# Block 1 without barriers around its recurrence, GELU beside the last set, and 14 of 16 gate matmuls behind the state inputs

## The chip, the cores and the metric

One core of one Trainium2 chip runs the whole program in one launch. The metric is the device time of that core in microseconds. The engines are TensorE (PE), VectorE (DVE), ScalarE (ACT), GpSimd (POOL) and SyncE (SP); each runs its own instruction stream and they meet only through semaphores. DMAs are issued from SP, ACT and POOL.

## What is computed

The model has three blocks on an activation of 1024 positions by 1024 channels, float32. The change lies in the first mixer of block 1, an S5 layer. Cut to what matters:

```
h = rmsnorm(x, norm_g[0])
branch, gate = split(h @ s5_w_in)            # 1024 -> 2 x 1024
# 64 groups of 16 channels drive 64 complex states each
h_t = lam_bar * h_{t-1} + b_bar @ u_t        # diagonal recurrence over 1024 positions
y_t = Re(C h_t) + D * u_t
y = gelu(y)
y = y * sigmoid(y @ s5_w_glu + s5_b_glu)
x = x + (y * silu(gate)) @ s5_w_out
```

What follows (the gating block, then block 2 with delta-rule and attention mixers, then block 3) is the same in both kernels.

## The kernel before

All activations are held transposed, channels on the partitions: eight tiles of 128 x 1024 in `c.X` (residual), `c.B` (normed input, later the GELU output y) and `c.C` (gate). One work area `c.W` is cut anew by every phase; its first 8192 columns are also `c.D`, eight tiles. A product of 1024 x 1024 by the activation is eight groups; a group is one output tile, made by 16 matmul instructions (eight k, two halves of 512 columns; each stands as two records in the trace) in `product_ct` (matmul at L161). Groups alternate between two halves of the PSUM tensor `products`: `start_group` waits until the group two before has been read (`group_read`), `take_group` waits until a group is done. Weights come in blocks of 512 KB through a ring of eight slots. SP's queue issues block n + 8 when the last group that uses block n is done.

The program is a list of phases. Every engine runs through the list in order. A phase added with `meet=True` ends in a barrier (L3568): each of the four compute engines drains, adds one to `phase_end` and waits for all four.

Four phases matter:

- **Norm.** `rms_phase` writes `c.B`.
- **`s5_input_phase`** (barrier behind it). ACT's queue loads the parameters. TensorE makes the eight branch tiles from `s5_w_in`, then turns C by eight transposes (L601) into one more group, `gp`. ACT copies each branch tile into one of four staging tiles (L617, the order of columns changed), then copies C (L620, L621). POOL stores each staged tile to `branch_dram` (L627) and at the end waits for all stores. VectorE makes b_bar, the powers of lam_bar, and a table of phases E in `c.C` (last of it at L636).
- **`s5_scan_phase`** (barrier behind it). The 64 groups go in eight sets of eight. The 1024 positions are cut into 128 steps of eight, so that a set needs one scan of 128 steps. For each set i: VectorE makes two filters, Pm and Q (L887, then `s5_pq_done`). TensorE transposes Pm (L827; ACT copies it to `into`, L867) and makes the kernel within eight steps from b_bar and Q (L839; ACT copies it to KK, L872). VectorE adds D on the diagonal (L942). POOL stores KK and loads it back eight times into the triangular `within` (L805, L809). TensorE makes the state inputs X from `into` and U (L847). U is the branch, loaded by POOL from `branch_dram` in eight DMAs a set (L792). VectorE turns X by E, scans (L953), turns back into H and signals `s5_h_done`; it goes on to the filters of set i + 1. TensorE meanwhile makes gate tile i (16 matmuls), then waits for H and `within` and makes the outputs (L857, L859). ACT copies them to Y (L878), which TensorE's next transposes wait for, and writes Silu of the gate tile to `c.C` (L880). POOL stores Y in eight DMAs (L814). At the end POOL waits for all stores of Y.
- **`s5_gate_phase`.** ACT's queue loads y back into `c.D` in four DMAs of two tiles (L985), ACT applies GELU to eight tiles into `c.B` (L992), TensorE waits for all eight, makes the eight GLU groups; ACT applies sigmoid (L997), VectorE multiplies `c.C` by y (L1014) and by the sigmoid (L1018, `s5_gated`); TensorE waits for all eight and makes the eight output groups.

Of the kernel before, what the change touches and what calls it, by code (L numbers as in the profile page):

```python
# [11 lines left out]
ACT = mybir.ActivationFunctionType  # L12
# [4 lines left out]
P = 128  # L17
# [133 lines left out]
def product_ct(c, pe, g, blocks, acts, ready=None):  # L151
# [12 lines left out]
    last.then_inc(c.group_done, 1)  # L164
# [386 lines left out]
def s5_input_phase(c, t, normed):  # L551
# [3 lines left out]
    b0 = len(c.plan.blocks)  # L555
    for m in range(KT):
        c.plan.add_blocks(columns(c, t["s5_w_in"][0], P * m, 1), g0 + m)
    c.plan.groups += KT
    gp = c.plan.groups
    c.plan.groups += 1  # L560
# [29 lines left out]
    def tensor(pe):  # L590
# [4 lines left out]
        for m in range(KT):  # L595
            product_ct(c, pe, g0 + m, [(b0 + m, KT, P)], [c.B[:, k, :] for k in range(KT)], normed if m == 0 else None)
        out = start_group(c, pe, gp)
        pe.wait_ge(c.s5_c_loaded, 16 * 16)
        for n in range(2):
            for q in range(4):  # L600
                last = pe.transpose(out[:, (4 * n + q) * P:(4 * n + q + 1) * P], craw[:, n, q, :], c.ident[:, :])  # L601
        last.then_inc(c.group_done, 1)

    def scalar(act):
# [8 lines left out]
        for m in range(KT):  # L613
            if m >= 4:
                act.wait_ge(c.branch_stored[m % 4], 16)
            got = take_group(c, act, g0 + m).rearrange("p (n s) -> p n s", s=S5_T)
            act.activation(stage[:, m % 4, :].rearrange("p (s n) -> p n s", s=S5_T), got, ACT.Copy)\  # L617
               .then_inc(c.group_read[(g0 + m) % 2], 1)
        got = take_group(c, act, gp)
        act.activation(s.CT[:, 0].rearrange("p j h -> p (j h)"), got[:, 0:BANK], ACT.Copy)  # L620
        act.activation(s.CT[:, 1].rearrange("p j h -> p (j h)"), got[:, BANK:], ACT.Copy, scale=-1.0)\  # L621
           .then_inc(c.group_read[gp % 2], 1)

    def gpsimd(pool):
        for m in range(KT):
            taken(c, pool, g0 + m)
# [120 lines left out]
def s5_scan_phase(c, t):  # L747
# [25 lines left out]
    Pm = area(2, JC, S5_T, S5_H)  # L773
    into = area(2, JC, P)
    Q = [area(2, JC, S5_T + 1, S5_H) for _ in range(2)]
    within = area(GC, S5_T * S5_H)
    KK = area(GC, S5_T * S5_H)
    r8 = area(JC, S5_N)
    U = [area(GC, S5_N) for _ in range(2)]
    T = area(2, JC, S5_N)  # L780
    Hh = area(2, JC, S5_N)
# [13 lines left out]
    def gpsimd(pool):  # L795
        pool.memset(within[:, :, :], 0.0).then_inc(c.pool_step, 1)
# [19 lines left out]
        pool.wait_ge(c.s5_y_stored, 16 * S5_T * S5_C)  # L816

    def tensor(pe):
        for i in range(S5_C):
            q = Q[i % 2]  # L820
            pe.wait_ge(c.s5_pq_done, i + 1)
# [19 lines left out]
            last.then_inc(c.s5_turned, 1)  # L841
            pe.wait_ge(c.s5_into_ready, 2 * i + 2)
# [7 lines left out]
            product_ct(c, pe, g0 + i, [(b0 + i, KT, P)], [c.B[:, k, :] for k in range(KT)])  # L850
# [10 lines left out]

    def scalar(act):
        for i in range(S5_C):
# [10 lines left out]

            act.wait_ge(c.s5_y_done, i + 1)
# [4 lines left out]
            act.activation(c.C[:, i, :], take_group(c, act, g0 + i), ACT.Silu).then_inc(c.group_read[(g0 + i) % 2], 1)  # L880

    def vector(dve):
# [5 lines left out]

        ch.done(dve.memset(H[:, :, :, 0:1], 0.0))
# [80 lines left out]
def s5_gate_phase(c, t):  # L970
# [8 lines left out]
    raw, y, gate = c.D, c.B, c.C  # L979
# [3 lines left out]
    def loads(sp):  # L983
        for m in range(0, KT, 2):
            sp.dma_start(raw[:, m:m + 2, :], c.y_dram[m * P:(m + 2) * P, :].rearrange("(k p) n -> p k n", p=P))\  # L985
              .then_inc(c.s5_y_loaded[m // 2], 16)

    def scalar(act):
        for m in range(KT):
            act.wait_ge(c.s5_y_loaded[m // 2], 16)  # L990

            act.activation(y[:, m, :].rearrange("p (n s) -> p s n", s=S5_T),  # L992
                           raw[:, m, :].rearrange("p (s n) -> p s n", s=S5_T), ACT.Gelu_apprx_tanh).then_inc(c.s5_y_gelu, 1)
# [8 lines left out]
    def tensor(pe):  # L1002
        pe.wait_ge(c.s5_y_gelu, KT)
        for m in range(KT):
            product_ct(c, pe, g0 + m, [(b0 + m, KT, P)], [y[:, k, :] for k in range(KT)])
        pe.wait_ge(c.s5_gated, KT)
        for m in range(KT):
            product_ct(c, pe, g0 + KT + m, [(b0 + KT + m, KT, P)], [gate[:, k, :] for k in range(KT)])
# [12 lines left out]
    phase = Phase(loads=loads, tensor=tensor, scalar=scalar, vector=vector)  # L1021
# [2351 lines left out]
def build(nc, t, out):  # L3373
    with ExitStack() as ctx:
# [165 lines left out]
        then(s5_input_phase(c, t, norm.normed), meet=True)  # L3540
        then(s5_scan_phase(c, t), meet=True)
# [124 lines left out]
```

## Time and profile before

| | us |
|---|---|
| Median of 3 runs | 4367.71 (4366.61 to 4369.51) |
| Profiled execution | 4361.82 |
| Its span | 4359.2 |
| TensorE busy | 4018.6 (92%) |
| VectorE busy | 1616.3 (37%) |
| ScalarE busy | 865.4 (20%) |
| GpSimd busy | 427.8 (10%) |

Times in the views are counted from the start of the span. The input phase of the mixer runs from about 50 to 178 us, the scan phase from 178 to 452, the gate phase from 452 to about 700. A bracket at the end of a timeline row tells how long the engine had been idle before and what ended the wait.
### The profile page before, as it was taken

The page shows a single profiled execution, that of the slowest core. Times are in us where ns is not written, and L with a number is a line of the kernel's source. Part 1 is how long each engine was busy: PE and PEld are TensorE (multiplying, and loading weights), DVE is VectorE, ACT ScalarE, POOL GpSimd, SP SyncE. Part 2 cuts the span into 40 slices and gives each one's busy share as a digit, 9 for nine tenths or more (in the row PEclk, how much of TensorE's full clock was granted, in tenths as well). Part 3 has the DMA queues.
Part 4 walks back from the last instruction along what each step waited for, and adds up shares of the span by engine and source line. Part 5 has one row for each costly group of instructions (what it writes and reads, how often), then busy time and mean ns, then how long its engine had stood idle before and what let it go on. Part 6 is the DMA issues. An engine that isn't in the chain of part 4 may idle for free.

```text
span 4359.2 us, 32122 instructions
## 1 busy us (share of the span) xinstructions
PE 4018.6 (92%) x13135; PEld 2033.6 (47%) x13135; DVE 1616.3 (37%) x2310; ACT 865.4 (20%) x971; POOL 427.8 (10%) x496
## 2 busy tenths in 40 slices
PE   5899699999999899987889999999989999989997
PEld 2455243454334567544434444444435554444553
DVE  6466113210233454134131434343443654324333
ACT  2111202200145221234120000000042431221122
POOL 0143000000000122012000222222200000000000
PEclk8999899999999999998999999999999999989998
DMA  4222111211101101110001111111111101003101
GB/s 117 66 66 55 64 38 40 53 29 39 34 15 34 40 24 40 34 49 20 27 20 51 39 48 39 48 39 49 39 29 25 29 14 35 20 13 97 29 10 44
DMA packets 291104, 174.49 MB, mean 40 GB/s; under 512 B 24096, under 2 KB 281999, under 8 KB 290703
## 3 DMA queue, kind: packets, MB, share of 16 engines
q1 hardware_dynamic: 253008, 126.47, 10.5%
q0 software_dynamic: 9856, 23.87, 2.0%
q10 hardware_dynamic: 28094, 22.11, 1.8%
q8 instruction: 105, 1.72, 0.2%
q14 instruction: 41, 0.33, 0.0%
HBM read 159.20 MB, written 13.21 MB: 40 GB/s over the span
## 4 chain that ended last, share of the span: by engine, by line
PE 53%; DVE 3%; ACT 2%; issue 1%; DMA 0%; POOL 0%; ACTq 0%; DVEq 0%
PE products L161 11%; PE products L278 9%; PE others L278 9%; PE products L2565 8%; PE products L2578 3%; PE others L2644 2%; PE products L1778 1%; PE products L179 1%; PE products L405 1%; PE products L1941 1%; PE others L1972 1%; PE products L1787 1%; PE products L3093 1%; PE products L3092 1%; PE others L1191 1%
## 5 line engine op out<-in xcount | busy, mean ns | idle before, releaser
L161 PE MATMUL products<-normed,weights 128*128 128x512 f32 x1728 | 759.1, 600 | 46.5 <-ACT normed L992 36.3
L161 PEld LDWEIGHTS products<-normed,weights 128*128 128x128 f32 x1728 | 330.7, 193 | 460.0 <-issue 451.1
L161 PE MATMUL products<-gate,weights 128*128 128x512 f32 x768 | 331.6, 593 | 5.0 <-DVE gate L1018 2.5
L2565 PE MATMUL products<-normed,weights 128*128 128x512 f32 (+2 forms) x704 | 321.8, 608 | 5.0 <-DVE normed L391 5.0
L161 PE MATMUL products<-residual,weights 128*128 128x512 f32 x672 | 295.6, 598 | 8.2 <-ACT residual L464 6.2
L161 PEld LDWEIGHTS products<-gate,weights 128*128 128x128 f32 x768 | 145.9, 190 | 188.9 <-issue 182.3
L161 PEld LDWEIGHTS products<-residual,weights 128*128 128x128 f32 x672 | 128.3, 192 | 170.6 <-issue 163.7
L2565 PEld LDWEIGHTS products<-normed,weights 128*128 128x128 f32 (+2 forms) x704 | 126.6, 187 | 163.9 <-issue 161.8
L179 PE MATMUL products<-weights,normed 128*128 128x512 f32 x384 | 167.5, 599 | 5.0 <-DVE normed L391 5.0
L278 PE MATMUL products<-gate,s_small 128*128 128x512 f32 x320 | 139.9, 592 | 0.0
L3361 POOL DMA_DIRECT2D out_dram<-work x8 | 4.3, 542 | 1214.3 <-ACT work L3350 1209.5
L1576 POOL TENSOR_TENSOR work<-work,levels 128x512 f32<-128x512 f32 x8 | 10.2, 1272 | 1130.7 <-DVE work L1702 1130.7
L179 PEld LDWEIGHTS products<-weights,normed 128*128 128x128 f32 x384 | 73.6, 192 | 99.3 <-issue 96.5
L288 POOL TENSOR_TENSOR s_small<-weights 128x512 f32<-128x512 f32 x32 | 41.4, 1295 | 798.0 <-PE products L161 305.9
L2644 PEld LDWEIGHTS others<-work 128*128 128x128 f32 (+1 forms) x1024 | 94.3, 195 | 47.8 <-issue 38.2
L1778 PE MATMUL products<-residual,weights 128*128 128x512 f32 x256 | 115.9, 600 | 0.0
L2644 PE MATMUL others<-work 128*128 128x128 f32 (+1 forms) x1024 | 98.7, 283 | 18.1 <-DVE work L2837 6.2
L1029 DVE TENSOR_TENSOR residual<-products,residual 128x1024 f32<-128x1024 f32 x24 | 29.4, 1224 | 229.0 <-PE products L161 220.2
L2578 PE MATMUL products<-weights,normed 128*128 128x512 f32 x256 | 111.5, 594 | 0.0
L161 PE MATMUL products<-work,weights 128*128 128x512 f32 x224 | 100.3, 605 | 4.9 <-DVEq L3568 4.9
L278 PEld LDWEIGHTS products<-gate,s_small 128*128 128x128 f32 x320 | 60.9, 190 | 76.4 <-issue 76.4
L2837 DVE COPY_PREDICATED work<-levels,others 128x1024 f32<-128x1024 int32 x56 | 73.0, 1304 | 39.2 <-PE others L2644 34.8
(543 smaller groups left out, 5641.9 us busy)
## 6 DMA issues: line engine op xcount, KB each, us to landing
weights<-in_w_in_dram SPq DMA_DIRECT2D x83, 512.0 KB, 3.8
weights<-in_w_up_dram SPq DMA_DIRECT2D x32, 512.0 KB, 4.2
weights<-in_w_down_dram SPq DMA_DIRECT2D x32, 512.0 KB, 5.0
weights<-in_sgu_w_in_dram SPq DMA_DIRECT2D x24, 512.0 KB, 3.8
weights<-in_s_w_in_dram SPq DMA_DIRECT2D x16, 512.0 KB, 4.0
weights<-in_w_out_dram SPq DMA_DIRECT2D x24, 256.0 KB, 2.9
work<-in_x_dram ACTq DMA_DIRECT2D x8, 512.0 KB, 10.1
branch_scratch<-work POOLq DMA_DIRECT2D x8, 512.0 KB, 2.9
```

Of the source, the lines that this page charges most:

```text
L161: last = pe.matmul(out[0:cols, half * BANK:(half + 1) * BANK], slot(c, b, kt, cols)[:, k, :], acts[n][:, half * BANK:(half + 1) * BANK], s ...
L179: last = pe.matmul(out[:, q * P:q * P + BANK], acts[k][:, tile * P:(tile + 1) * P], wide[:, :, k, :], start=(k == 0), stop=(k == KT - 1))
L278: last = pe.matmul(self.bank[n], w[:, k * P:(k + 1) * P], moving[k], start=(k == 0), stop=(k == KT // 2 - 1))
L405: last = pe.matmul(out[:, h * BANK:(h + 1) * BANK], c.mean_mat[:, :], c.tmp[:, k % 2, h * BANK:(h + 1) * BANK], start=(k == 0), stop=(k == ...
L1191: last = pe.matmul(out[:, h * BANK:(h + 1) * BANK], c.mean_mat[:, :], squares[:, h * BANK:(h + 1) * BANK], start=True, stop=True)
L1778: last = pe.matmul(o[:, 0:BANK], slot(c, f.b, KT, P)[:, kk, :], x[kk][:, half * BANK:(half + 1) * BANK], start=(kk == 0), stop=(kk == KT - 1))
L1787: last = pe.matmul(o[:, 0:BANK], x[kk][:, f.n * P:(f.n + 1) * P], wide[:, :, kk, :], start=(kk == 0), stop=(kk == KT - 1))
L1941: pe.matmul(L[e][:, x:y], q[half(e), a, i * P:(i + 1) * P], k[half(e), a, x:y], start=True, stop=(y < w))
L2565: last = pe.matmul(out[0:cols, half * BANK:(half + 1) * BANK], slot(c, f.b, kt, cols)[:, kk, :], acts[kk][:, half * BANK:(half + 1) * BANK ...
L2578: last = pe.matmul(out[:, 0:BANK], x[kk][:, f.n * P:(f.n + 1) * P], wide[:, :, kk, :], start=(kk == 0), stop=(kk == KT - 1))
L2644: last = pe.matmul(pair(j + h)[:, i * P:(i + 1) * P], K[rows(u, h), i * P:(i + 1) * P], Q[rows(u, h), i * P:(i + 1) * P], start=True, stop ...
L2837: ch.done(dve.copy_predicated(o, mask, got), *reader(j))
```

## The change

Both barriers around the scan phase are dropped. What they ordered is ordered by waits and by a new layout of `c.W`:

- In the input phase the group `gp` with the turned C moves from the end to between branch products 3 and 4, on TensorE and ACT, and the group numbers are shifted accordingly. In the scan VectorE waits for C's copy, ACT and POOL for the stores of the branch, and POOL clears `within` only when set 0's filters are done.
- The work area of the scan is laid out so that the parts that set 7 still uses (Q[1], U[1], `within`, H, Y) lie behind the first seven tiles of `c.D`.
- In the scan, the gate product of set i is issued by a generator: one matmul before the wait for the filters, one after the kernel products, 14 behind the state inputs. The number of matmuls is the same.
- In the last set, ACT waits for H, then issues the loads of y's tiles 0 to 6 in three DMAs, takes Silu of the last gate tile and GELU of tiles 0 to 2, and only then copies the outputs to Y. GELU of tiles 3 to 7 follows. Tile 7 is loaded by POOL behind its own stores.
- In the gate phase TensorE waits for one GELU tile at a time in the first GLU group, and for one gated tile at a time in the first output group.

```diff
@@ product_ct
-                pe.wait_ge(c.normed, ready + n + 1)
+                pe.wait_ge(c.normed if on is None else on, ready + n + 1)
@@ s5_input_phase
+    gm = [g0 + m + (1 if m >= 4 else 0) for m in range(KT)]
+    gp = c.s5_c_group = g0 + 4
...
         for m in range(KT):
-            product_ct(c, pe, g0 + m, ..., normed if m == 0 else None)
-        out = start_group(c, pe, gp)
-        pe.wait_ge(c.s5_c_loaded, 16 * 16)
-        for n in range(2):
-            for q in range(4):
-                last = pe.transpose(...)
-        last.then_inc(c.group_done, 1)
+            if m == 4:
+                out = start_group(c, pe, gp)
+                ...                               # the same eight transposes
+            product_ct(c, pe, gm[m], ..., normed if m == 0 else None)
@@ scalar: the two copies of C move to m == 4 likewise
@@ s5_scan_phase, layout of c.W
     Pm = area(2, JC, S5_T, S5_H)
+    T = area(2, JC, S5_N)
+    Q = [area(2, JC, S5_T + 1, S5_H)]
+    r8 = area(JC, S5_N)
     into = area(2, JC, P)
+    Hh = area(2, JC, S5_N)
+    KK = area(GC, S5_T * S5_H)
+    U = [area(GC, S5_N)]
     within = area(GC, S5_T * S5_H)
+    U.append(area(GC, S5_N))
+    Q.append(area(2, JC, S5_T + 1, S5_H))
     H = area(2, JC, S5_N)
     Y = area(GC, S5_N)
@@ gpsimd
+        pool.wait_ge(c.s5_pq_done, 1)
         pool.memset(within[:, :, :], 0.0).then_inc(c.pool_step, 1)
...
         pool.wait_ge(c.s5_y_stored, 16 * S5_T * S5_C)
+        pool.dma_start(c.D[:, KT - 1, :], c.y_dram[(KT - 1) * P:KT * P, :]).then_inc(c.s5_y_loaded[3], 16)
@@ tensor
+    def gates(pe):
+        for i in range(S5_C):
+            out = start_group(c, pe, g0 + i)
+            block_ready(c, pe, b0 + i)
+            for k in range(KT):
+                for half in range(HALVES):
+                    last = pe.matmul(...)
+                    if k < KT - 1 or half < HALVES - 1:
+                        yield
+            last.then_inc(c.group_done, 1)
+            yield
...
+            advance(1)
             pe.wait_ge(c.s5_pq_done, i + 1)
...                                               # transposes, kernel products
+            advance(1)
             pe.wait_ge(c.s5_into_ready, 2 * i + 2)
...                                               # state inputs
-            product_ct(c, pe, g0 + i, [(b0 + i, KT, P)], [c.B[:, k, :] for k in range(KT)])
+            advance(14)
             pe.wait_ge(c.s5_h_done, i + 1)
@@ scalar
+    def gelu(act, m):
+        act.wait_ge(c.s5_y_loaded[min(m // 2, 2) if m < KT - 1 else 3], 16)
+        act.activation(c.B[:, m, :]..., c.D[:, m, :]..., ACT.Gelu_apprx_tanh).then_inc(c.s5_y_gelu, 1)
+
     def scalar(act):
+        for k in range(4):
+            act.wait_ge(c.branch_stored[k], 32)
...
+            if i == S5_C - 1:
+                act.wait_ge(c.s5_h_done, S5_C)
+                act.wait_ge(c.s5_y_stored, 16 * S5_T * i)
+                act.wait_ge(c.s5_kk_stored, 16 * S5_C)
+                for n, (lo, hi) in enumerate(((0, 2), (2, 4), (4, KT - 1))):
+                    act.dma_start(c.D[:, lo:hi, :], c.y_dram[lo * P:hi * P, :]...)\
+                       .then_inc(c.s5_y_loaded[n], 16)
+                act.activation(c.C[:, i, :], take_group(c, act, g0 + i), ACT.Silu).then_inc(...)
+                for m in range(3):
+                    gelu(act, m)
             act.wait_ge(c.s5_y_done, i + 1)
...
+        for m in range(3, KT):
+            gelu(act, m)
@@ vector
+        taken(c, dve, c.s5_c_group)
+        ch.wait()
@@ s5_gate_phase: its loads and its GELU loop are gone
-        pe.wait_ge(c.s5_y_gelu, KT)
         for m in range(KT):
-            product_ct(c, pe, g0 + m, [(b0 + m, KT, P)], [y[:, k, :] for k in range(KT)])
-        pe.wait_ge(c.s5_gated, KT)
+            product_ct(c, pe, g0 + m, [(b0 + m, KT, P)], [y[:, k, :] for k in range(KT)],
+                       0 if m == 0 else None, c.s5_y_gelu)
         for m in range(KT):
-            product_ct(c, pe, g0 + KT + m, ..., [gate[:, k, :] for k in range(KT)])
+            product_ct(c, pe, g0 + KT + m, ..., [gate[:, k, :] for k in range(KT)],
+                       0 if m == 0 else None, c.s5_gated)
@@ build
-        then(s5_input_phase(c, t, norm.normed), meet=True)
-        then(s5_scan_phase(c, t), meet=True)
+        then(s5_input_phase(c, t, norm.normed))
+        then(s5_scan_phase(c, t))
```

## Rows read from the trace of the kernel before

**Rows 1.** The page, busy time of each engine with its share.
```profile
PE 4018.6 (92%) x13135; PEld 2033.6 (47%) x13135; DVE 1616.3 (37%) x2310; ACT 865.4 (20%) x971; POOL 427.8 (10%) x496
```

**Rows 2.** Stretches: length, busy of each engine (instructions), granted clock, DMA share, GB/s.
```profile
197.10:219.30 22.20, 22.20 (x82) 12.61 (x80) 20.67 (x34) 0.00 (x0) 4.19 (x8) 1.00 0.17 41
219.30:228.10 8.80, 6.47 (x73) 5.03 (x72) 0.56 (x2) 5.26 (x5) 7.39 (x15) 0.81 0.45 90
435.50:471.80 36.30, 0.00 (x1) 0.00 (x0) 8.61 (x8) 18.36 (x12) 4.16 (x8) 0.51 0.38 130
471.80:488.40 16.60, 16.57 (x33) 7.29 (x34) 1.19 (x1) 1.24 (x1) 0.00 (x0) 0.84 0.00 0
```

**Rows 3.** The barriers' line: POOL's drains, duration ns min/median/max.
```profile
L3568 POOLq DRAIN  x7: 41/1399/8962, 177.5 to 3134.7; - x7
```

**Rows 4.** Timeline, input to set 0: start us, us, engine, line, work, [idle before].
```profile
60.14 112.06 PE L161 MATMUL products<-normed,weights 128*128 128x512 f32 x256
172.04 1.04 PE L601 MATMUL products<-ident,work 128*128 128x128 f32 x8
...
117.31 1.98 ACT L617 ACTIVATE work<-products 128x1024 f32<-128x1024 f32 x1 [11.75 <-PE products L161]
...
174.51 0.53 POOL L627 DMA_DIRECT2D branch_scratch<-work  x1 [13.19 <-ACT work L617]
...
179.58 8.39 POOL L792 DMA_DIRECT2D work<-branch_scratch  x16 [0.30 <-POOL work L796]
...
178.30 0.07 DVE L889 MEMSET work<- 128x8 f32 x1 [47.48 <-POOLq L3568]
```

**Rows 5.** Timeline, set 0 to 1 on TensorE, VectorE, POOL; kernel products of set 7.
```profile
220.56 1.47 PE L827 MATMUL others<-ident,work 128*128 128x128 f32 x8 [1.21 <-ACT work L878]
221.96 3.15 PE L839 MATMUL others<-work,s_small 64*16 64x128 f32 x32
226.23 1.97 PE L847 MATMUL others<-work 128*64 128x128 f32 x32 [1.12 <-ACT work L872]
228.13 14.00 PE L161 MATMUL products<-normed,weights 128*128 128x512 f32 x32
...
228.25 2.87 DVE L887 TENSOR_TENSOR work<-others,gate 128x512 f32<-128x512 f32 x4 [1.44 <-PE others L847]
...
237.93 1.41 DVE L887 TENSOR_TENSOR work<-work 128x508 f32<-128x508 f32 x2
...
248.86 0.88 DVE L887 TENSOR_TENSOR work<-work 128x256 f32<-128x256 f32 x2
...
231.47 4.18 POOL L809 DMA_DIRECT2D work<-within_scratch  x8 [1.93 <-DMA within_scratch<-work]
...
407.84 2.39 PE L839 MATMUL others<-work,s_small 64*16 64x128 f32 x32
```

**Rows 6.** Timeline, last set to the first GLU product.
```profile
435.54 1.02 ACT L878 ACTIVATE work<-others 128x1024 f32<-128x1024 f32 x1 [24.25 <-PE others L859]
...
436.85 4.16 POOL L814 DMA_DIRECT2D y_scratch<-work  x8 [17.08 <-ACT work L878]
451.72 2.06 ACTq L985 DMA_DIRECT2D work<-y_scratch  x4
...
456.64 15.09 ACT L992 ACTIVATE normed<-work 128x1024 f32<-128x1024 f32 x8 [1.54 <-DMA work<-y_scratch]
...
471.83 3.75 PE L161 MATMUL products<-normed,weights 128*128 128x512 f32 x4 [36.33 <-ACT normed L992]
```

**Rows 7.** DMA issues, 170 to 480 us: issue, count, KB each, median us to landing.
```profile
work<-branch_scratch POOLq DMA_DIRECT2D x64, 64.0 KB, 2.6
...
y_scratch<-work POOLq DMA_DIRECT2D x64, 64.0 KB, 2.3
...
branch_scratch<-work POOLq DMA_DIRECT2D x1, 512.0 KB, 2.9
```

**Rows 8.** Timeline, first group of the output product.
```profile
587.07 13.14 PE L161 MATMUL products<-gate,weights 128*128 128x512 f32 x30 [2.52 <-DVE gate L1018]
```

More of the change, by code:

```diff
@@ L595, in tensor @@
         for m in range(KT):
-            product_ct(c, pe, g0 + m, [(b0 + m, KT, P)], [c.B[:, k, :] for k in range(KT)], normed if m == 0 else None)
-        out = start_group(c, pe, gp)
-        pe.wait_ge(c.s5_c_loaded, 16 * 16)
-        for n in range(2):
-            for q in range(4):
-                last = pe.transpose(out[:, (4 * n + q) * P:(4 * n + q + 1) * P], craw[:, n, q, :], c.ident[:, :])
-        last.then_inc(c.group_done, 1)
+            if m == 4:
+                out = start_group(c, pe, gp)
+                pe.wait_ge(c.s5_c_loaded, 16 * 16)
+                for n in range(2):
+                    for q in range(4):
+                        last = pe.transpose(out[:, (4 * n + q) * P:(4 * n + q + 1) * P], craw[:, n, q, :], c.ident[:, :])
+                last.then_inc(c.group_done, 1)
+            product_ct(c, pe, gm[m], [(b0 + m, KT, P)], [c.B[:, k, :] for k in range(KT)], normed if m == 0 else None)
     def scalar(act):
@@ L816, in gpsimd, with advance @@
         pool.wait_ge(c.s5_y_stored, 16 * S5_T * S5_C)
+        pool.dma_start(c.D[:, KT - 1, :], c.y_dram[(KT - 1) * P:KT * P, :]).then_inc(c.s5_y_loaded[3], 16)
[5 more added lines that the diff above has]
+                for half in range(HALVES):
+                    last = pe.matmul(out[:, half * BANK:(half + 1) * BANK], slot(c, b0 + i, KT, P)[:, k, :],
+                                     c.B[:, k, half * BANK:(half + 1) * BANK], start=(k == 0), stop=(k == KT - 1))
+                    if k < KT - 1 or half < HALVES - 1:
+                        yield
+            last.then_inc(c.group_done, 1)
+            yield
     def tensor(pe):
+        work = gates(pe)
+        def advance(n):
+            for _ in range(n):
+                next(work)
         for i in range(S5_C):
             q = Q[i % 2]
+            advance(1)
             pe.wait_ge(c.s5_pq_done, i + 1)
@@ L978, in s5_gate_phase @@
     c.plan.groups += 2 * KT
-    raw, y, gate = c.D, c.B, c.C
+    y, gate = c.B, c.C
     sig = c.tmp
     sums = Sums(c)
[L983 to L986, printed above, removed]
     def scalar(act):
[L989 to L993, printed above, removed]
         for m in range(KT):
@@ L1002, in tensor @@
     def tensor(pe):
[L1003 removed]
         for m in range(KT):
[L1005 to L1006 removed]
+            product_ct(c, pe, g0 + m, [(b0 + m, KT, P)], [y[:, k, :] for k in range(KT)],
+                       0 if m == 0 else None, c.s5_y_gelu)
         for m in range(KT):
[L1008 removed]
+            product_ct(c, pe, g0 + KT + m, [(b0 + KT + m, KT, P)], [gate[:, k, :] for k in range(KT)],
+                       0 if m == 0 else None, c.s5_gated)
     def vector(dve):
@@ L1019, in vector @@
         add_to_residual(c, dve, g0 + KT, sums)
-    phase = Phase(loads=loads, tensor=tensor, scalar=scalar, vector=vector)
+    phase = Phase(tensor=tensor, scalar=scalar, vector=vector)
     phase.sums = sums
```

36 lines of the change are left out of this document (17 added, 19 removed).

## The prediction

> **What bounds the kernel now.** I read the page first: TensorE is busy 92% of the span [rows 1], so only stretches in which it idles, or runs at the lower clock, can give time back. The mean by stages then shows where block 1 stands apart [rows 2]: TensorE works 22.2 of 22.2 us at the full clock through one set's gate product and output products, 6.47 of 8.80 us in the turn to the next set at a granted clock of 0.81, and not at all in the 36.3 us after the last set, after which the first GLU product takes 16.6 us at 0.84. Elsewhere such a product takes 13.85 us (14.00 less the modelled tail of the last matmul) [rows 5]. The rest of the program is not touched and moves along as a whole.
>
> Last I followed the time order of each engine through the three places where block 1 waits: input to set 0 [rows 4], one set to the next [rows 5], last set to the GLU products [rows 6]. The POOL row of the barriers' line gives the size of one hidden cost: one of its drains takes 8962 ns [rows 3].
>
> **Input to set 0.** Before: the last input product ends at 172.2, its copy is stored from 174.51, VectorE starts set 0's filters only at 178.30 after 47.48 us of waiting for POOL's drain, and the gate product of set 0 starts at 197.1. After: VectorE finished the phase tables at 130.8 (178.30 - 47.48 [rows 4]) and C is read by about 120.5, so the filters (10.4 us, as below) are ready near 141, far ahead. What is late next is the branch. The turn of C (1.04 us [rows 4]) now stands between input products 3 and 4. It also costs a wait: product 4 reuses product 3's bank pair, whose copy runs 117.31 to 119.25, while TensorE is through with C at 118.2. So 1.04 + 1.05 = 2.1 us is put on the chain: last store at 176.6 instead of 174.51. It lands 2.9 later [rows 7], 179.5; then memset and gap as before (1.3, from 178.30 to 179.58), first branch load 180.8, the eighth issued 7 x 0.53 = 3.7 later, landed after 2.6 [rows 7]: 187.1. ScalarE's two copies (from 179.5, 2 us) and POOL's wait for the filters lie inside that; set 0's kernel store waits behind 16 loads, until 189.3, and its way home (1.93 + 4.18 + 2.0 = 8.1 us [rows 5]) ends at 197.9, before the output products at 202. State inputs run 187.2 to 189.2 (1.97 us), 8.0 us ahead of 197.1. Of the gate product only 14 of 16 matmuls stand behind them: 2 x 0.866 = 1.73 saved. But TensorE has been idle some 8 us by then, so I charge the cold start that the first GLU product shows, 16.6 - 13.85 = 2.75. Sum: 8.0 + 1.7 - 2.7 = **7.0 us**. Bounds: without the cold start 9.7; with state inputs at half speed as well (another 2) 5.
>
> **Seven set-to-set rounds.** A round lasts (435.45 - 219.36)/7 = 30.87 us (ends of the output products, from the starts of what follows them [rows 5, 6]) and TensorE is in all of it: 13.85 gate, 8.4 outputs (22.2 - 13.85), 1.20 waiting for ScalarE's copy of the outputs, 1.40 transposes, 3.15 kernel products, 1.12 waiting for ScalarE's copy of these, 1.9 state inputs [rows 2, 5]. The change puts one gate matmul (0.87 us) into each wait. They fit: 0.87 < 1.12. That alone takes 1.73 off. The second part is the clock: 219.3 to 228.1 was granted 0.81, and once TensorE does not stop there, the dip may go. Transposes at the full clock took 1.04 [rows 4] against 1.47, and the kernel products in the one set that met the dip late took 2.39 against 3.15 [rows 5]: up to 1.2 us more, so a round of 27.9.
>
> VectorE's chain is the floor under that: 11.1 us from state inputs to state (228.25 to 239.34), 10.3 for the next filters (239.44 to 248.86 + 0.88), then 1.1 transposes, 1.9 to 2.4 kernel products, 1.0 copy and 2.0 state inputs, with handovers 27.7 us. The state itself (11.1) must be there when 14 matmuls (12.1) are through: it is, by 1.0 us, and that is what 16 less 2 leaves. POOL: its kernel rows landed at 237.6 (231.47 + 4.18 + 2.0) when the outputs started at 242; of those 4.4 us 3 are taken, 1.4 are left. So all three chains are within 1.5 us of each other, and I take 28.4 for a round, nearer the floor than 29.1. 7 x 2.5 = **17.5 us**. Bounds: 7 x 1.7 = 12 (dip stays) to 7 x 3.1 = 22 (floor); below 12 only if a late row or state is waited for, which these margins exclude as a rule.
>
> **Last set to GLU.** Before: outputs done 435.45, stores issued from 436.85, last one issued 3.6 later and landed after 2.3 [rows 7], 442.8; the loads are issued at 451.72, which is the 8.96 us drain [rows 3, 6]. First GELU 456.64, eight take 15.09, TensorE starts at 471.83 and ends product 0 at 488.4: 52.95 us after the outputs.
> After, counted from the end of the last set's state inputs: state 11.1; three loads issued by ScalarE, the first landed 4.92 later (451.72 to 456.64), 16.0. In between Silu (1.02, at 12.2 when the gate product is through) and one table load (1.28) are hidden. GELUs 0 to 2: 3 x 1.89, 21.7. Outputs end at 12.1 + 8.4 = 20.5, and the copy of Y waits behind those GELUs until 21.7 (1.2 late, the price of this order). From that copy's start 7.25 us to the last landing (435.54 to 442.8): 29.0; POOL's load of the last tile, 512 KB like the branch stores that took 2.9 [rows 7]: 32.0. GELUs 3 to 6 end at 30.3 beside it, GELU 7 at 33.9. TensorE follows tile by tile and has 14 of product 0's 16 matmuls behind it by about 32.2; two more after the last GELU, and 1 us for a short stop before: 36.6, or 16.1 after the outputs. 52.95 - 16.1 = **36.9 us** (of it 9.0 the drain, 2.7 the cold clock, 12.1 product 0 ahead, 13 the loads and GELUs beside the set). Bounds: 38.5 with the copy of Y in time and no stop; 27 if POOL keeps its 9 us.
> VectorE's eight gate multiplications (L1014) follow the GELUs and end 1.3 us after the last, long before the first sigmoid's product. SP issues the same weight loads on the same groups.
>
> A rule to hold against this: POOL's seven drains took 41 ns at least, 1399 in the median and 8962 at most [rows 3]. The Trainium skill, "VectorE: DVE Perf Modes", section "The DRAIN you can't avoid", knows the drains of the runtime's preamble as some 12 ns each, constant. By that a barrier costs nothing and the 9 us would belong to something else that stays; the median row is a hundred times that, so I count the 9 us as the barrier's; by the page the sum would be 54.9 and the time 4313.
>
> **GLU to output product.** TensorE waits 2.52 us for the last gated tile [rows 8]; with a wait per tile seven others stand before it: **2.5 us** (2 to 3).
>
> **Sum.** 7.0 + 17.5 + 36.9 + 2.5 = 63.9 us. The profiled execution took 4361.8 (span 4359.2 and 2.6 around it) and becomes 4297.9; the median of the three runs is 5.9 higher, 4367.7, so I predict 4304.
>
> **Rivals.**
> The clock's dip stays: gate matmuls fill 0.87 of each wait but transposes and kernel products run as slow as now. For it: the dip is there in every round though the wait is only 1.2 us. Against: that wait shrinks to 0.3. Rounds of 29.1: 17.5 becomes 12.3, so 4309.
> POOL keeps its 9 us: the long drain is work owed for its 64 x 3 DMA issues, and now stands in front of the load of the last tile. For it: the drain before it, with 8 issues behind it, was much shorter, as the store of 174.51 and the load of 179.58 enclose it. Against: in every round POOL issues its kernel loads as soon as the store before them has landed, 1.93 us [rows 5], with no debt to be seen. TensorE would then idle 11 us more and meet the cold clock (2.7): 4304 + 9 + 2.7 = 4316.
> Slower: the scattered gate matmuls fail to hold the clock and sets run at the half level. Gate matmuls then take 27.4 instead of 13.7 a set, 110 us over eight: 4304 + 110 = 4414. It outweighs the gain from 64/13.7 = five such sets on. Against: output products follow the gate matmuls now as then, at 1.00 [rows 2].
> The change doesn't do what it says: the last set's loads cannot start early because the stores of the set before are late. They land near 2 us after its state inputs, nine before they are needed; no chance of its own.
>
> **How the numbers follow.** Forecast 0.68, dip stays 0.16, POOL's 9 us 0.10, slower 0.03, the remaining 0.03 on losses that I do not see and that eat the gain. All low terms give 5 + 12 + 27 + 2 = 46 (4322), all high ones 9.7 + 22 + 38.5 + 3 = 73 (4295); both ends at once are unlikely, so the range is 4295 to 4321, and the forecast's own 4297 to 4311. 0.2% is 8.7 us, the least that counts as a difference here. Faster 0.95, same 0.02, slower 0.03.
>
> **What would show it.** Input: copy of C at about 119, TensorE idle 1 us there; filters of set 0 before 142; state inputs at 187, not 195. Rounds: a period of 28.4 and a granted clock near 1.00 in the turn; with 0.81 there and 29.1 the dip stayed. TensorE waiting for VectorE's state or for POOL's kernel rows would mean that a margin of 1.0 or 1.4 us was wrong. End: first GELU before the outputs end, the last load of Y's rows 32 us after the state inputs, product 0 finished 16 us after the outputs. The forecast is wrong if POOL stands still between the landed stores and that load, if a round stays above 29.5, or if anything after block 1 gives back time.

## The result

| | before | changed |
|---|---|---|
| Median, us | 4367.16 (4 runs, 4363.94 to 4369.51) | 4303.03 (4 runs, 4300.96 to 4306.13) |
| Profiled execution, us | 4361.82 | 4302.76 |
| Its span, us | 4359.2 | 4300.9 |

The ratio is 0.9854, 95% interval 0.9837 to 0.9871. Predicted was 4304 us, range 4295 to 4321.

Stretches of the changed kernel, columns as in [rows 2]: the wait of set 0 with its state inputs, the 14 gate matmuls behind them, the turn from set 0 to 1, then the time from the last outputs to the last GELU, and the end of GLU product 0.

```profile
187.40:191.10 3.70, 3.66 (x33) 3.36 (x33) 0.00 (x0) 0.00 (x0) 2.52 (x5) 0.50 0.58 124
191.10:204.30 13.20, 13.20 (x30) 5.95 (x30) 12.56 (x17) 0.00 (x0) 4.17 (x8) 0.92 0.10 22
212.60:219.80 7.20, 6.99 (x78) 4.75 (x77) 0.87 (x4) 5.13 (x5) 5.80 (x12) 1.00 0.47 83
407.40:422.40 15.00, 12.31 (x30) 5.25 (x29) 7.29 (x7) 12.28 (x8) 4.75 (x9) 0.98 0.53 150
422.40:425.80 3.40, 3.40 (x5) 1.61 (x6) 1.18 (x1) 1.23 (x1) 0.00 (x0) 0.57 0.00 0
```

The turn is 7.2 us at the full clock where 8.8 us at 0.81 stood [rows 2], two gate matmuls included. The 36.3 us without TensorE are gone: it works 12.3 of the 15.0 us after the outputs.

Rows of TensorE's timeline from the input phase to set 1; compare them with [rows 4, 5]:

```profile
116.83 1.04 PE L601 MATMUL products<-ident,work 128*128 128x128 f32 x8
119.05 55.20 PE L161 MATMUL products<-normed,weights 128*128 128x512 f32 x128 [1.18 <-ACT work L623]
...
187.44 3.68 PE L874 MATMUL others<-work 128*64 128x128 f32 x32 [8.54 <-DMA work<-branch_scratch]
...
212.58 1.13 PE L830 MATMUL products<-normed,weights 128*128 128x512 f32 x2
213.85 1.06 PE L853 MATMUL others<-ident,work 128*128 128x128 f32 x8
214.84 1.93 PE L865 MATMUL others<-work,s_small 64*16 64x128 f32 x32
216.71 1.12 PE L830 MATMUL products<-normed,weights 128*128 128x512 f32 x2
217.90 1.97 PE L874 MATMUL others<-work 128*64 128x128 f32 x32
```

One gate matmul (two records) sits in each of the two waits (212.58 and 216.71). Transposes take 1.06 and kernel products 1.93, where [rows 5] had 1.47 and 3.15. TensorE stops 1.18 us behind the turned C, and 8.54 us for set 0's branch rows, after which the state inputs run at half speed.

The end of the scan, ScalarE's and POOL's timelines of the changed kernel; compare them with [rows 6]:

```profile
398.18 1.45 ACTq L914 DMA_DIRECT2D work<-y_scratch  x3
399.68 1.02 ACT L916 ACTIVATE gate<-products 128x1024 f32<-128x1024 f32 x1 [14.69 <-PE products L830]
400.72 1.28 ACT L891 ACT_TABLE_LOAD   x1
403.35 5.81 ACT L891 ACTIVATE normed<-work 128x1024 f32<-128x1024 f32 x3 [1.34 <-DMA work<-y_scratch]
408.96 1.05 ACT L922 ACTIVATE work<-others 128x1024 f32<-128x1024 f32 x1
409.92 7.67 ACT L891 ACTIVATE normed<-work 128x1024 f32<-128x1024 f32 x4
420.29 2.03 ACT L891 ACTIVATE normed<-work 128x1024 f32<-128x1024 f32 x1 [2.71 <-DMA work<-y_scratch]
...
425.84 1.11 ACT L1036 ACTIVATE work<-products,vectors 128x1024 f32<-128x1024 f32 x1 [2.22 <-PE products L161]
```
```profile
410.30 4.17 POOL L819 DMA_DIRECT2D y_scratch<-work  x8 [16.93 <-ACT work L922]
416.49 0.59 POOL L822 DMA_DIRECT2D work<-y_scratch  x1 [2.02 <-DMA y_scratch<-work]
```

POOL issues the load of the last tile 2.02 us after its last store: no drain stands before it any more. The drain itself has not gone away. A timeline leaves drains out; the barriers' line of the changed kernel shows POOL's:

```profile
L3607 POOLq DRAIN  x5: 41/1706/9673, 416.5 to 3076.2; - x5
```

The first one starts at 416.5, beside that load, belongs to the next barrier on POOL's list and takes 9.67 us. No engine waits for it: the other engines reach that barrier only after 1385 us. So the change has moved the drain out of the path, not removed it. The first sigmoid starts at 425.84 instead of 488.45.

Term by term, from the two traces:

| | predicted | measured | from |
|---|---|---|---|
| Input to set 0's outputs | 7.0 | 6.7 | copy of Y 219.40, 212.68 |
| Seven rounds | 17.5 | 21.3 | that copy to the last outputs' end, 216.05, 194.73 |
| Outputs to first sigmoid | 36.9 | 34.6 | 53.0, 18.4 |
| Last sigmoid's start to output product | 2.5 | 2.7 | 2.43, -0.26 |
| Sum | 63.9 | 65.3 | output product starts at 587.07, 521.78 |

The two spans differ by 58.3 only. The rest is given back far behind block 1, in a stretch with the same 1000 matmuls of block 2's attention in both kernels, before and changed:

```profile
1903.00:2189.00 286.00, 239.97 (x1005) 125.82 (x1005) 96.25 (x249) 97.61 (x200) 49.84 (x68) 0.91 0.07 22
```
```profile
1838.00:2130.60 292.60, 244.62 (x1001) 125.34 (x1000) 95.87 (x247) 97.51 (x200) 49.82 (x68) 0.90 0.07 22
```

This stretch took 283 to 293 us in the profiles of all kernels run here, 293 with the variant of the old kernel below too, and as little as 283 with a variant of the changed one, so it does not follow the change. A second place varies as well: the last stretch of the program, from POOL's last barrier drain on (3076.2 here), took 1218 to 1225 us. That is why single times scatter by some 10 us and why I compare block 1 by its own marks below. The medians differ by 64.1.

### The profile page after: what moved, and what is told of

Same layout as the page of the kernel before. It is cut to its first block, busy times and chain, and to the rows that moved or that the text cites. A ratio compares the mean times of both kernels' runs of the same rounds, so it can differ in the third digit from the quotient of the medians.

```text
span 4300.9 us, 32114 instructions
## 1 busy us (share of the span) xinstructions
PE 4016.9 (93%) x13135; PEld 2024.6 (47%) x13135; DVE 1615.4 (38%) x2310; ACT 865.3 (20%) x971; POOL 428.1 (10%) x497
## 4 chain that ended last, share of the span: by engine, by line
PE 53%; DVE 3%; ACT 2%; issue 1%; DMA 0%; POOL 0%; ACTq 0%; DVEq 0%
PE products L161 12%; PE products L278 9%; PE others L278 9%; PE products L2604 8%; PE products L2617 3%; PE others L2683 2%; PE products L1817 1%; PE products L179 1%; PE products L405 1%; PE products L1980 1%; PE others L2011 1%; PE products L1826 1%; PE products L3132 1%; PE products L3131 1%; PE others L1230 1%
## 5 line engine op out<-in xcount | busy, mean ns | idle before, releaser
L161 PEld LDWEIGHTS products<-normed,weights 128*128 128x128 f32 x1472 | 281.5, 192 | 368.0 <-issue 352.6
## 6 DMA issues: line engine op xcount, KB each, us to landing
work<-in_x_dram ACTq DMA_DIRECT2D x8, 512.0 KB, 10.4
```

## The experiments

All are compared by the trace: X is the start of state inputs, a round the time from one X to the next (counted from set 1 on, since set 0 starts cold), "outputs" the end of a set's output products.

**How the gate matmuls are spread.** One, one and 14 in the changed kernel.

```diff
             q = Q[i % 2]
-            advance(1)          # a, before the wait for the filters
+            advance(a)
...
-            advance(1)          # b, after the kernel products
+            advance(b)
...
-            advance(14)         # c, behind the state inputs
+            advance(c)
```

a, b, c = 0, 0, 16:

> The changed kernel with all 16 gate matmuls of a set behind its state inputs, none in the two waits; everything else of the change stays. Theory (the two matmuls fill the waits and by that also keep the clock): the round from set to set goes from 27.8 back to about 30.9 us (1.7 for the matmuls, 1.2 for the clock, whose dip returns at 0.81 in the turn), so the kernel is some 21 us slower than the changed one, near 4324. Rival A (the matmuls fill, but the dip went with the barriers or the new layout): rounds of 29.5, clock at 1.00 in the turn, 4315. Rival B (VectorE's chain was always the floor): rounds stay within 0.5 of 27.8, 4305.

Measured: rounds of 30.72 to 30.86 and 4313.82 us, median of 4 runs (4307.64 to 4319.89), ratio to the kernel before 0.989 (0.9872 to 0.9907). The turn from set 1 to 2, and TensorE in it:

```profile
243.70:252.50 8.80, 6.47 (x75) 5.22 (x73) 0.62 (x3) 3.98 (x4) 7.20 (x14) 0.81 0.45 87
```
```profile
245.16 1.94 PE L853 MATMUL others<-ident,work 128*128 128x128 f32 x8 [1.21 <-ACT work L922]
247.03 2.52 PE L865 MATMUL others<-work,s_small 64*16 64x128 f32 x32
250.66 1.97 PE L874 MATMUL others<-work 128*64 128x128 f32 x32 [1.12 <-ACT work L906]
```

The dip is back, with the same two waits and the same 0.81 as before the change, without any barrier. So the spreading, not the layout or the missing barriers, removed it here. (Two open waits do not bring it without fail: see the kernel before with seven drains, below.) Block 1 is 18.2 us longer (first sigmoid at 443.99); the medians differ by less, 10.8, with runs 12 us apart.

a, b, c = 1, 0, 15:

> One gate matmul before the wait for the filters, none after the kernel products, 15 behind the state inputs. Theory (the wait before the transposes is the one after which the clock fell): no dip, the wait after the kernel products is open again at 1.1 us, a round of 27.8 + 0.87 - 0 = 28.6, and the kernel near 4309. Rival (either open wait brings the dip): a round of 29.8 with 0.8 granted in the turn, 4317.

Measured: rounds of 28.55, 4293.74 us (one run). TensorE in the turn from set 1 to 2:

```profile
241.49 1.12 PE L830 MATMUL products<-normed,weights 128*128 128x512 f32 x2
242.76 1.06 PE L853 MATMUL others<-ident,work 128*128 128x128 f32 x8 [0.15 <-ACT work L922]
243.75 1.94 PE L865 MATMUL others<-work,s_small 64*16 64x128 f32 x32
246.81 1.97 PE L874 MATMUL others<-work 128*64 128x128 f32 x32 [1.12 <-ACT work L906]
```
```profile
241.50:249.50 8.00, 6.73 (x77) 4.94 (x77) 1.91 (x6) 3.98 (x4) 6.59 (x13) 1.00 0.47 90
```

The second wait is open by 1.12 us and the clock stays at 1.00, so the second wait alone does not bring the dip. Whether the first alone does, with the second filled, no run shows. The matmul before the transposes is worth 30.8 - 28.55 = 2.3 us a round, the one after the kernel products 0.87, which is its own length. The time of the whole is 9 us below the changed kernel's, with block 1 2.9 us longer: the attention stretch again (286 against 293).

a, b, c = 2, 1, 13:

> Two gate matmuls before the wait for the filters, one after the kernel products, 13 behind the state inputs. Theory (VectorE's chain from state inputs to filters, 11.1 + 10.3, and on through TensorE is the floor of a round at 27.7): the round stays at 27.7 to 27.8 though the output products start 0.9 earlier after the state inputs, and TensorE waits about 0.4 us before the transposes. Rival (TensorE's own chain sets the round): it falls to 27.3 and the kernel by 3 us. Second rival (the state is late for 13 matmuls): the round grows by what TensorE waits for it.

Measured: rounds of 27.64, 4299.01 us (one run). The output products start 0.87 earlier and the round does not follow. VectorE's chain is the floor, as the theory had it. VectorE's last filter operation and TensorE in the turn from set 2 to 3:

```profile
268.78 0.89 DVE L934 TENSOR_TENSOR work<-work 128x256 f32<-128x256 f32 x2
```
```profile
267.77 1.98 PE L830 MATMUL products<-normed,weights 128*128 128x512 f32 x4
269.72 1.09 PE L853 MATMUL others<-ident,work 128*128 128x128 f32 x8
```

The filters end at 269.67 and the transposes start at 269.72. The two gate matmuls before them take 1.73 us in the stream (to 269.50), so about 0.2 us of waiting is hidden in their modelled tail, half of the 0.4 that I named. The kernel rows came late in one round here too (0.84 us of waiting, a round of 28.43).

**The drain.** The changed kernel with one in front of the last load:

```diff
         pool.wait_ge(c.s5_y_stored, 16 * S5_T * S5_C)
+        pool.drain()
         pool.dma_start(c.D[:, KT - 1, :], ...)
```

> The changed kernel with one drain of GpSimd between its wait for the last stores of Y and its load of the last tile. Theory (the 9 us before were the barrier's drain itself, owed for some 200 DMA issues since the drain before it, and nothing of it shows where no drain stands): the drain takes 8 to 10 us here, the load of the last tile is issued that much later, TensorE idles 9 us more before the last two matmuls of GLU product 0 and the kernel is 9 to 11 us slower, 4313. Rival (the 9 us came from the meeting of the four engines): the drain takes under 1 us and nothing moves.

The drain's row:

```profile
L822 POOLq DRAIN  x1: 8975/8975/8975, 416.0 to 416.0; - x1
```

8975 ns against 8962 at the barrier [rows 3]. First sigmoid at 435.17 instead of 425.84, 9.3 later. The whole, 4303.78 us (one run), does not show it: some 4 us came back in the attention stretch and 7 in the last 1220 us of the program, which vary from one execution to the next as said above. There is no meeting of engines here, so the time is the drain's own. What is owed goes to whichever drain comes next: the barrier's drain behind this one took 3.87 us instead of 9.67.

The kernel before with a drain in every set but the last:

```diff
                                Y[s_ * S5_H:(s_ + 1) * S5_H, :, :]).then_inc(c.s5_y_stored, 16)
+            if i < S5_C - 1:
+                pool.drain()
```

> The kernel before with a drain of GpSimd behind the stores of Y in each of sets 0 to 6; both barriers stay. Theory (a drain costs what has been issued since the last one: 0.72 us after 8 DMAs, 8.96 after 200, so some 0.04 each): each of the seven takes 1 to 2.5 us, hidden under POOL's 4.4 us of room in a set, the one of the second barrier falls from 8.96 to about 1 and the loads of y start 7 to 8 us earlier after the last copy of Y. Rival (a fixed cost of a drain after scattered stores, whatever was issued before): seven drains of about 9 us, POOL's kernel rows come late in every set and the kernel loses some 4 us a set. Second rival (a cost of this one place): seven short drains and 8.96 at the barrier as before.

The new line and the barriers' line:

```profile
L817 POOLq DRAIN  x7: 3596/3884/3926, 225.9 to 408.3; - x7
```
```profile
L3570 POOLq DRAIN  x7: 41/1392/2521, 179.1 to 3130.5; - x7
```

No barrier's drain is over 2521 ns any more; the one behind the scan took 1.4 us, and first sigmoid follows the last copy of Y by 45.9 us instead of 52.9: 7.0 us won with seven instructions. The whole took 4356.65 us against 4369.12 of the kernel before on the same chip (one run each, and single times scatter by some 10 us, so the 7.0 rests on the marks). So the debt theory holds in kind, not in my 0.04 us per DMA: the seven take 3.6 to 3.9, of which by my estimate some 2 are the landing of the stores that they stand behind (2.3 [rows 7]), and the first, with 33 DMAs since the drain before it, takes no longer (3.86) than those with 25; the sum of eight drains, 28.4 us, is more than the 9 that they replace, only hidden.

This run also limits what can be said of the clock. Its turns from set 0 to 1 and from set 2 to 3:

```profile
219.90:228.70 8.80, 6.48 (x81) 5.29 (x80) 1.70 (x6) 5.13 (x5) 4.17 (x8) 1.00 0.35 61
281.80:290.60 8.80, 7.30 (x75) 5.75 (x76) 1.54 (x4) 3.19 (x4) 4.97 (x10) 0.82 0.34 61
```

Both waits stand open (1.21 and 1.12 us) in every turn, yet the clock stayed at 1.00 in the first two and fell from the third on.

**The barrier behind the input, put back.**

```diff
-        then(s5_input_phase(c, t, norm.normed))
+        then(s5_input_phase(c, t, norm.normed), meet=True)
```

> The changed kernel with the barrier behind the input phase put back. Theory (the start of set 0 is 8 us earlier because filters, transposes and kernel products are done while the branch is stored and loaded): the filters of set 0 start only near 180.4, state inputs near 197, the first copy of Y at 220 to 221 instead of 212.7, and what follows is unmoved: 7 to 8 us slower. Rival (the branch's load was the limit anyway): state inputs stay within 2 us of 187.4.

Measured: X at 200.00, first copy of Y at 222.47 (9.8 later than 212.68), 4311.56 us (one run). 3 us later than I expected, by a wait that the change added: POOL's clearing and its branch loads stand behind the filters.

```profile
192.29 1.11 POOL L801 MEMSET work<- 128x1024 f32 x1 [13.71 <-DVE work L934]
...
193.70 8.39 POOL L796 DMA_DIRECT2D work<-branch_scratch  x16 [0.30 <-POOL work L801]
```

In the changed kernel the filters end at 141 and that wait is free; with the barrier it makes set 0 even later than before (X at 195.21 there). So about 3 of the 9.8 us belong to that wait and not to the barrier itself.

**The branch rows earlier.** Set 0's rows go to Y's area.

```diff
@@ s5_input_phase, gpsimd, in the loop over m
             pool.dma_start(c.branch_dram[m * P:(m + 1) * P, :], ...)
+            if m == 5:
+                c.s5_first_inputs(pool)    # waits for set 0's filters and branch tiles 0, 1; loads sets 0, 1
@@ s5_scan_phase
-        for k in range(4):                 # ScalarE
+        for k in range(3):
             act.wait_ge(c.branch_stored[k], 32)
```

> The changed kernel with the branch rows of sets 0 and 1 loaded between the stores of branch tiles 5 and 6 (set 0's rows, which lie in tile 0, go to the area of Y, which is free until set 0's outputs are copied), and ScalarE waits only for the stores of three staging tiles, since the fourth lies outside what it writes. Theory (set 0 waits for nothing but this load, 8.54 us, and pays the half clock for it): state inputs start at about 179 instead of 187.4, take 1.97 instead of 3.68, the gate matmuls behind them 12.1 instead of 13.2, and the first copy of Y comes at 201 to 202, 11 us earlier. Rival (set 0 then waits for POOL's kernel rows, whose store follows the clearing of the triangle at 180.7): the copy comes only at 206 or later, 6 us gained.

TensorE behind set 0's kernel products:

```profile
178.59 1.13 PE L842 MATMUL products<-normed,weights 128*128 128x512 f32 x2
179.78 1.97 PE L886 MATMUL others<-work 128*64 128x128 f32 x32
181.68 12.29 PE L842 MATMUL products<-normed,weights 128*128 128x512 f32 x28
```

X at 179.78 without a wait, at full speed; copy of Y at 202.25, 10.4 earlier, as the theory said. 4283.18 us (one run). The granted clock was 1.00 from 65 to 628 us. The first sigmoid came 12.7 us earlier (413.09), 2.3 more than this edit explains: 0.7 in the round with the late kernel rows, 1.6 at the end, where this run kept its clock behind the stop for the last GELU:

```profile
411.00:414.50 3.50, 3.43 (x8) 1.63 (x9) 1.49 (x2) 2.41 (x3) 0.00 (x0) 1.00 0.04 12
```

**GELU and the copy of Y.** None ahead of the copy, then two:

```diff
-                act.activation(c.C[:, i, :], take_group(c, act, g0 + i), ACT.Silu)...
-                for m in range(3):
-                    gelu(act, m)                       # Silu and all eight after the copy of Y
```

> The changed kernel with Silu and all eight GELUs of the last set behind the copy of Y (the loads stay where they are). Theory (what the end gains is the missing barrier and the loads beside the set; the three GELUs ahead give back part of their worth because the copy of Y and its stores wait for them): the copy starts right behind the outputs, 1.3 us earlier after them than in the changed kernel, the last tile is there 1.3 us earlier, but the last GELU ends only after Silu, table load and eight GELUs, 19 us after the outputs; TensorE follows tile by tile. First sigmoid 20.5 to 21.5 us after the outputs instead of 18.4: 2 to 3 us slower. Rival (GELU beside the set carries the end): three times 1.9 and Silu come on top, 7 us or more.

Measured: first sigmoid 21.6 us after the outputs (18.4 in the changed kernel), 4299.82 us (one run). TensorE stops 5.46 us for the first GELU, and none later; its clock was at the half level for 6.8 us around that stop.

```diff
-                for m in range(3):
+                for m in range(2):
```

> The changed kernel with two GELUs ahead of the copy of Y instead of three. Theory: the copy is in time (1.3 us earlier), the last tile and with it the last GELU as much earlier, and TensorE stops for 1.3 us instead of 2.7; if that also spares it the half clock for the last matmuls, the first sigmoid comes 3 us earlier after the outputs (15.4 instead of 18.4), if not, 1.3 (17.1). Rival: the seventh GELU now ends later than the last tile lands, so nothing is gained.

Measured: 37.9 us from the last X to the first sigmoid, against 40.8: 2.9 won, TensorE's stop 0.91 us and the clock at 1.00, the better of the two cases; 4298.54 us (one run). But the clock's part of it is no proof for this order. The run with early branch rows and three GELUs also kept its clock, behind a stop of 2.55 us, and took 39.2 from the last X to the first sigmoid. Against that one, two GELUs win 1.3 us; that much the experiment shows. In the same run one round took 34.4 us instead of 28.7. TensorE in that set, then the round before and the round of 34.4:

```profile
315.92 0.46 PE L884 MATMUL others<-work 128*128 128x128 f32 x2 [0.73 <-DMA work<-within_scratch]
```
```profile
288.00:315.90 27.90, 26.98 (x150) 15.89 (x149) 21.42 (x37) 3.98 (x4) 13.04 (x25) 1.00 0.30 70
...
315.90:350.30 34.40, 34.32 (x158) 21.68 (x158) 21.20 (x37) 3.98 (x4) 13.02 (x25) 0.80 0.25 57
```

TensorE waited 0.73 us for POOL's kernel rows and then ran at a mean of 0.80 for a whole round. The changed kernel waits there too (below) and kept its clock.

**The output product waits for all tiles, as before.**

```diff
+        pe.wait_ge(c.s5_gated, KT)
         for m in range(KT):
             product_ct(c, pe, g0 + KT + m, ...)
```

> The changed kernel in which TensorE waits for all eight gated tiles before the output product, as before. Theory: it stops 2.5 us there again, and the time from the last sigmoid to the output product grows by 2.5; nothing else moves. Rival (the weights of the output product or the bank pair are late anyway): no difference.

```profile
524.69 5.75 PE L161 MATMUL products<-gate,weights 128*128 128x512 f32 x9 [2.52 <-DVE gate L1057]
```

2.52 us, to the hundredth what [rows 8] had; 2.43 after the last sigmoid's start instead of -0.26. One thing more moved than I expected: here the clock was at 0.50 for the 3.3 us behind the stop, which in the kernel before, at the same stop, it was not. 4303.63 us (one run).

**Two GLU products together.**

```diff
+        for m, ks in ((0, range(KT - 1)), (1, range(KT - 1)), (0, (KT - 1,)), (1, (KT - 1,))):
+            for k in ks:
+                pe.wait_ge(c.s5_y_gelu, k + 1)
+                ...                                    # both halves of group m, tile k
```

> The changed kernel with GLU products 0 and 1 made together: k = 0 to 6 of both, then k = 7 of both. Theory (TensorE stops 2.69 us for the last GELU and then runs its last matmuls at the half clock): no stop and no clock below 1.00 from set 1 to the end of the GLU products; product 1 is finished 4.6 us earlier after the last outputs. Rival (the stop only moves, because the GELUs come one every 1.9 us while TensorE needs 1.75 for a tile): under 2 us gained.

TensorE behind the last outputs:

```profile
407.09 27.73 PE L1049 MATMUL products<-normed,weights 128*128 128x512 f32 x64
```

No idle, 64 records at the full clock while the last GELU ends at 422.0. Second sigmoid at 434.86 against 439.58: 4.4 us after allowing for the copy of Y, 0.3 earlier here. 4285.68 us (one run).

**Both improvements at once.**

> Early loads of the first two sets' branch rows and GLU products 0 and 1 made together, both at once on the changed kernel. The two lie 200 us apart and touch no common wait, so their gains add: 10.4 for the start of set 0, 4.4 at the end, clock at 1.00 from the input products to the end of the GLU products; 15 us faster than the changed kernel, near 4288, and a ratio to the kernel before of 0.982. If one of the gains were only moved, less than 12.

```profile
64.60:560.00 495.40, 492.67 (x1857) 253.84 (x1857) 253.35 (x484) 81.60 (x70) 110.23 (x210) 1.00 0.26 69
```

TensorE is busy 492.7 of 495.4 us at a granted clock of 1.00. The last sigmoid of the GLU comes at 507.42 against 522.04, 14.6 earlier for 10.4 + 4.4. Median 4283.22 us (5 runs, 4271.78 to 4288.82) against 4365.64 (9 runs); ratio 0.981, 0.9793 to 0.9827, below the interval of the changed kernel. This version beats both the kernel before and the changed one. By whole times it can't be told from either improvement alone (4283.18 and 4285.68, one run each); that the gains add is shown by the marks of block 1.

## Why the prediction was right

The sum came out at 65.3 against 63.9 and the median within 1 us. Luck had a part in that, twice. The terms' errors (-0.3, +3.8, -2.3, +0.2) cancel. And the profiled execution, from which the sum was taken off, came out at 4302.8 and not at 4297.9, because stretches behind block 1 gave 7 us back; the two medians happened to lie 64.1 apart. The prediction named time given back behind block 1 as a sign that it was wrong. It was given back, and the sign misled, since those stretches vary whatever the kernel.

**Input to set 0** was right step by step: C's turn and the wait behind it (1.18 for 1.05), the stores' landing, state inputs at 187.44 for 187.2. The cold start fell on the state inputs (3.68 instead of 1.97) more than on the gate matmuls (13.2 instead of 12.1): 2.8 us, charged at 2.75.

**The rounds** were mis-sized: I took 28.4, between a dip that stays and the floor; they ran at the floor, 27.69, which I had put at 27.7. The step that failed is the choice between the bounds. A misreading went the same way. I took 2.39 us for kernel products nearly free of the dip, in a set that met it late. But set 7 met it early, its transposes took 1.94 us, all at the half level:

```profile
405.97 1.94 PE L827 MATMUL others<-ident,work 128*128 128x128 f32 x8 [1.20 <-ACT work L878]
```

At the full clock they take 1.06 and 1.93, so the dip cost 1.3 us in that turn and 1.6 in the first [rows 5], and not up to 1.2. The dip went completely, and the spreading did it (0, 0, 16 brings it back; 1, 0, 15 does not). One round took 28.69. In it POOL paused 2.15 us between the fourth and fifth kernel load, and TensorE waited 0.77 us for them. POOL and TensorE of the changed kernel:

```profile
307.83 2.26 POOL L814 DMA_DIRECT2D work<-within_scratch  x4 [1.93 <-DMA within_scratch<-work]
312.24 2.09 POOL L814 DMA_DIRECT2D work<-within_scratch  x4 [2.15 <-issue]
```
```profile
315.92 0.46 PE L884 MATMUL others<-work 128*128 128x128 f32 x2 [0.77 <-DMA work<-within_scratch]
```

So the margin of 1.4 us that I left POOL is right as a margin, and one pause of 2.15 overran it. The pause could have been read before the prediction: it stands in the same place of the kernel before, where POOL had the room for it, and I had taken POOL's margin from one set only.

```profile
328.53 2.09 POOL L809 DMA_DIRECT2D work<-within_scratch  x4 [1.97 <-issue]
```

In the kernel before, the changed one and nine of the variants it comes before POOL's 130th DMA of the program; in the two with the early branch rows before the 146th (1.6 us). The kernel with seven drains is the only one without it. What it is, and whether it is the same work that a drain does, no run shows.

**The end** fell short by 2.3. GELU takes 1.92 to 1.94 apiece, not 1.89. The last tile's load took 3.8 from its issue to the GELU, not 3.0. And the stop for it, 2.69 us, was followed by 3.4 us at 0.57 for the last matmuls, where I had charged 1 us in all. The drain was 9.0 of this term: shown by the 8975 ns of the inserted one. The rival that POOL's debt would stall its next DMA instead is refuted by 2.02 us from store to load; the debt was paid by POOL's next drain, 9.67 us, which nobody waits for. The 12 ns that the Trainium skill ("VectorE: DVE Perf Modes", "The DRAIN you can't avoid") gives for the preamble's drains do not carry over: no drain behind DMAs here was below 0.7 us. GELU ahead of the copy of Y is worth little in itself: 3.2 us for three, and 1.3 more for two at equal clock. That leaves some 22 of the 34.6 us. By the timelines they lie with the loads beside the set, with TensorE following tile by tile (12.3 us of product 0 done before the last GELU) and with the clock; no experiment here parts the three.

**The output product**: 2.5 for 2.7.

That the clock would stay down, and that nothing would be gained, did not happen.

## What to carry to other kernels

Before a barrier is counted as the wait of the slowest engine, read its drains: on an engine that issues many DMAs the drain itself can be the longest part, and waits on the few things really shared move it to where nobody waits for it. Independent matmuls are best spent one by one in the short waits of a dependent chain: one of 0.87 us in the right gap was worth 2.3, since it also kept the clock. Read a margin in every turn of a loop and not in one: the pause that cost 1 us here was in the trace from the start. When chains are level to within a microsecond, the next gain lies at the ends, where one operand per tile lets the product start before the last.

## What the runs showed of the hardware that was not expected

- A drain of GpSimd took 0.72 us behind 8 DMAs and 1.4 behind 17, all of them landed; 3.6 to 3.9 behind 25 to 33 with the last 8 in flight; 8.96 and 8.98 behind some 200, all landed. With no drain in the path it was paid later, 9.67 us at the next one. DMAs are not all that a drain costs: in the kernel before, the four barrier drains with no DMA since the drain before took 41 ns, 46 ns, 1.4 and 1.7 us, and the 1399 ns that the prediction set against the preamble's 12 ns is one of these.
- TensorE's clock is not settled by the length of a stop. In the same round, it fell after a stop of 0.73 us in one run (a mean of 0.80 over the next 34.4 us) and not after stops of 0.64 to 0.84 us in six others. At the last GELU it fell after 2.54, 2.63 and 2.69 us and not after 2.55 and 2.79. With no matmul in the waits it fell in all seven turns of two kernels (0.81 over 8.8 us) and in the last five of a third, not in its first two; with the first wait filled and 1.12 us open in the second it never fell (one run).
- Block 2's attention, unchanged in all kernels, took between 283 and 293 us from one execution to the next (granted 0.91 in the 286 us and 0.90 in the 292.6 us shown). No run shows what sets it.
